# A deeper retention pipeline under the last projection pieces, and a last stage whose vector work runs by pairs of heads

## The chip, the cores and the metric

One core of a Trainium2 chip runs the whole program. The metric is the device time of one execution in microseconds (us); lower is better. The median of three executions of the kernel before is 3984.34 us (3983.41 to 3984.66). The engines are TensorE (PE, with its weight loads as PEld), VectorE (DVE), ScalarE (ACT), GpSimd (POOL) and SyncE (SP, which only issues loads here).

## What is computed

Two layers of a model with four parallel branches run over 18 tiles of 128 tokens (256 tokens of context, 2048 latent ones). Cut to what matters:

```python
h = rmsnorm(x) * (1 + scale) + shift
q, k, v, gate, ... = split(h @ w_in)          # 1024 -> 4096 columns
o_a, o_b = window attention, neighbourhood attention
o_c = retention(q, k, v)                      # linear attention with fixed decays, both ways
o_d = hgrn2(q, z_f, z_b, v)                   # the same with decays from the data, both ways
x = x + gate * rmsnorm(concat(o * silu(g)) @ w_out)
```

Each recurrence runs forwards and backwards and carries one 64x64 state per head. Within a 128-token tile, `o_c` is a product of queries and keys, masked by a fixed decay matrix, plus two products with the states. In `o_d` the decay differs in every channel, so the products of queries and keys inside a 64-token block are taken in seven levels (distances of 1, 2, 4, ... tokens), each with keys and queries scaled by its own decays. All data are fp32, and every matrix product is done in fp32.

## The kernel before

A layer has stages. A first stage projects 36 pieces (a piece is one tile by 512 columns, eight matmuls of 128x512). The window and neighbourhood attentions follow, with 72 further pieces laid between their matmuls and 4 projected ahead. The last two stages are the ones that the change touches.

**The retention stage** has `BACK_SLOTS` = 38 slots, numbered m. It projects the 32 pieces that are left, in alternation 6 (decays) and 7 (gates and values), in slots 0 to 33. `NO_PIECE = (6, 12)` leaves two slots without a piece, so `REST_END`, the last slot with one, is 33. TensorE works one piece ahead: the matmuls of the piece of slot m+1 fill the gaps of slot m (`fill`). Around them a slot holds

- in slots 0 to 17, one tile of the backward retention: `back_ret` on VectorE (rotate and decay the keys), the state product on TensorE, `back_state` on VectorE;
- in slots 2 to 37, half a tile of the backward hgrn2 (`back_hg_sums`, `decay_back`, `back_keys_hg`, `back_hg`). `BACK_AT` = 2 says where that begins;
- in slots 18 to 35 (`FORE` = 18), the forward retention tile j = m - 18: TensorE takes the state product (`keys_ret`) and the outputs of two pairs of heads (`outputs_ret`), VectorE subtracts the mean and adds up the state (`centred_ret`), and the tile after it is prepared: GpSimd rotates two tiles ahead (`rope_ret`), TensorE transposes (`turn_ret(j+1)`) and forms scores (`scores_ret(j+1)`) at the end of the slot, and VectorE masks the scores (`masked_ret(j)`) at the start of the next slot.

In slots 34 and 35 (`REST_END` + 1 and + 2) VectorE also makes the levels 0 to 1 and 2 to 6 of the first hgrn2 tile. In slot 36 TensorE forms its weights, and in slot 37 VectorE masks them.

**The last stage** runs over n = 1 to 19. In an iteration VectorE makes the seven levels of tile n (`level_hg`, four operations each, three in the last), and between them masks and adds up the level products of tile n-1 (`masked_hg`, once for each of four heads: one multiply of 448 columns out of PSUM, one reduction to 64), then finishes the residual of tile n-3 and the gating of tile n-1. ScalarE copies the weights of each head into one matrix (`weights_out`). GpSimd makes the decayed keys and the sum of both keys (`keys_hg`), clears the table of decays for tile n+1 (`clear_decays`), and stores results. TensorE forms the level products (`weights`), the outputs (`weigh`), transposes, and the output projection of tile n-2 (sixteen matmuls of 128x512, `fill` again).

Every engine runs its own queue in the order written, and waits on semaphores. `ps[:, 4:6]` holds the level products, one bank for each head of a pair, so a second pair waits until ScalarE has read the first.

Of the kernel before, what the change touches and what calls it, by code (L numbers as in the profile page):

```python
# [13 lines left out]
P = 128  # L14
# [162 lines left out]
NO_PIECE = (6, 12)  # L177
# [156 lines left out]
HG_CORE = 14 * GW + P + 2 * P + 4 * GW + 4 + 12 * P + 16 * P + 8 * LEVELS * P + 8 * P + 4 * P + 128 + (SLOTS + 1) * 64  # L334
# [20 lines left out]
def build(nc, ins, outs):  # L355
# [142 lines left out]
    with ExitStack() as s:  # L498
# [11 lines left out]
        hg.ks = sb(s, "hg_ks", [P, 2, 2, P])  # L510
# [4 lines left out]
        hg.w = sb(s, "hg_w", [P, SLOTS + 1, 64])  # L515
# [78 lines left out]
    for a, name in ((ret, "ret"), (hg, "hg")):  # L594
# [78 lines left out]
    def _(sp):  # L673
# [22 lines left out]
        for l in range(DEPTH):  # L696
# [217 lines left out]
            for m in range(BACK_SLOTS):  # L914
# [5 lines left out]
                if 0 <= m - FORE + 3 < NT:  # L920
                    load_ret(m - FORE + 3)
# [51 lines left out]
    def _(pool):  # L973
        for l in range(DEPTH):
# [156 lines left out]
            for n in range(NT + 3):  # L1131
# [13 lines left out]
    def _(pe):  # L1145
# [3 lines left out]
        for l in range(DEPTH):  # L1149
# [328 lines left out]
            def weights(t, g):  # L1478

                b, u = t % 2, l * NT + t  # L1480
                if g == 0:
                    pe.wait_ge(hg.qk_ready, u + 1)
                    pe.wait_ge(hg.ks_ready, u + 1)
# [15 lines left out]
                product(SLOTS, hg.ks[:, b, g], hg.xT[:, b, g])  # L1499
# [46 lines left out]
            for m in range(BACK_SLOTS):  # L1546
# [19 lines left out]
                if 0 <= j + 1 < NT:  # L1566
                    turn_ret(j + 1)
# [14 lines left out]
                if 0 <= j + 1 < NT:  # L1582
                    scores_ret(j + 1)
# [38 lines left out]
    def _(act):  # L1622
# [37 lines left out]
        for l in range(DEPTH):  # L1660
# [214 lines left out]
            def weights_out(t, h):  # L1875
                u = l * NT + t
                act.wait_ge(hg.tc_ready, HEADS * u + h + 1)
                need(act, hg.o_done, 2 * u + h // 2)
                for blk in range(2):
                    at, other = slice(blk * 64, (blk + 1) * 64), slice((1 - blk) * 64, (2 - blk) * 64)  # L1880
                    nc.scalar.activation(hg.p[at, h % 2, at], hg.tc[at, h % 2, :], ACT.Copy)
                    last = nc.scalar.activation(hg.p[at, h % 2, other], ps[at, 4 + h % 2, (SLOTS + 1) * 64:(SLOTS + 2) * 64],
                                                ACT.Copy)
                last.then_inc(hg.p_ready, 1)
# [13 lines left out]
            for m in range(BACK_SLOTS):  # L1898
# [8 lines left out]
                if 0 <= j + 1 < NT:  # L1907
                    take_ret(j + 1)
                if 0 <= j < NT:
                    square(j)  # L1910
                if REST_AT[m] and REST_AT[m][0] == 6:
                    bounds_ln(*REST_AT[m])
                if m in (REST_END + 1, REST_END + 2):
                    take_decays(m - REST_END - 1)
# [667 lines left out]
```

## Time and profile before

| what | value |
|---|---|
| time, median of three | 3984.34 us |
| the profiled execution: its time / its span | 3983.12 us / 3981.3 us |
| TensorE busy (share of the span) | 3793.2 us (95%) |
| VectorE busy | 2382.4 us (60%) |
| ScalarE busy | 1237.6 us (31%) |
| GpSimd busy | 572.8 us (14%) |
| first weights of the last stage masked, layer 2 | at 3542.62 us |
| one iteration of the last stage, VectorE | 3699.59 to 3722.70 us |

The profiled time lies 1.8 us above its span and 1.2 us below the median of the runs. Busy shares are means over stages with different limits, so the text reads the two changed stages in order of time. All starts are counted from the start of the span; the rows are of the second layer, whose code is that of the first.

### The profile page before, as it was taken

The numbers are of one execution on the slowest core, as the hardware profiler recorded it, in microseconds if no ns is written. First come the engines' busy times: TensorE is split into PE (matmuls) and PEld (weight loads), VectorE is DVE, ScalarE is ACT, GpSimd is POOL, SyncE is SP. The second block draws the span as 40 slices with busy tenths as digits, with TensorE's granted clock in tenths as the row PEclk, the third lists the DMA queues.
The fourth block names the chain that finished last, engine by engine and source line by source line (L and its number), as shares of the span: only waits on it lengthen the run. The fifth ranks groups of instructions, "written<-read, shape, count | busy, mean of one in ns | idle before, by whom it ended". The sixth has DMA issues, their size and how long they took to land. (4 is left out here: it accounts for less than half of the span.)

```text
span 3981.3 us, 63647 instructions
## 1 busy us (share of the span) xinstructions
PE 3793.2 (95%) x24449; PEld 2062.0 (52%) x24449; DVE 2382.4 (60%) x4811; ACT 1237.6 (31%) x3545; POOL 572.8 (14%) x870
## 2 busy tenths in 40 slices
PE   7999999999999998899999999999999989979998
PEld 4544555555554455555544455554555545555554
DVE  2334345224667887899932333551256688889996
ACT  3311232233331122445542023232333212224544
POOL 2000000100000354100100000001000005521100
PEclk9999999999999998999999999999999999979999
DMA  7432121222223334322332121213222233333322
GB/s 243 145 139 96 51 67 50 92 75 70 89 81 107 116 106 140 117 97 96 129 117 87 48 89 54 74 39 119 76 79 75 87 107 114 113 133 108 116 96 71
DMA packets 234365, 388.92 MB, mean 98 GB/s; under 512 B 30000, under 2 KB 150032, under 8 KB 233936
## 3 DMA queue, kind: packets, MB, share of 16 engines
q1 hardware_dynamic: 194096, 262.55, 20.8%
q0 software_dynamic: 39968, 122.30, 8.5%
q8 instruction: 195, 3.19, 0.3%
q14 instruction: 106, 0.87, 0.1%
HBM read 264.42 MB, written 122.25 MB: 97 GB/s over the span
## 5 line engine op out<-in xcount | busy, mean ns | idle before, releaser
L1184 PE MATMUL ps<-w_sb,hT 128*128 128x512 f32 x4608 | 2193.0, 609 | 3.7 <-ACT hT L1681 2.4
L1184 PEld LDWEIGHTS ps<-w_sb,hT 128*128 128x128 f32 x4608 | 812.5, 191 | 764.5 <-issue 725.7
L1539 PE MATMUL ps<-wo_sb,mT 128*128 128x512 f32 x1152 | 537.5, 606 | 3.4 <-ACT mT L1851 3.4
L980 POOL DMA_DIRECT2D projected<-row_t x252 | 138.6, 550 | 2461.4 <-DVE row_t L2087 1084.4
L2084 DVE RECIPROCAL e_t<-e_t 128x256 f32<-128x256 f32 (+1 forms) x180 | 430.7, 2393 | 6.2
L1539 PEld LDWEIGHTS ps<-wo_sb,mT 128*128 128x128 f32 x1152 | 207.1, 191 | 209.2 <-issue 198.1
L2082 DVE TENSOR_SCALAR e_t<-e_t 128x256 f32<-128x256 f32 (+1 forms) x180 | 71.3, 396 | 226.0 <-ACT row_t L1699 194.9
L1693 ACT ACTIVATE row_t<-ps 128x512 f32<-128x512 f32 x108 | 64.5, 597 | 393.5 <-PE ps L1184 387.8
L2191 DVE TENSOR_REDUCE nei_st<-ps 128x2 f32<-128x512 f32 x72 | 49.8, 691 | 209.7 <-PE ps L1294 209.7
L2224 DVE COPY win_pT<-ps 128x512 f32<-128x512 f32 x64 | 44.3, 692 | 213.2 <-PE ps L1303 213.2
L2224 DVE COPY nei_pT<-ps 128x512 f32<-128x512 f32 x64 | 44.3, 691 | 207.8 <-PE ps L1303 207.8
L2191 DVE TENSOR_REDUCE win_st<-ps 128x2 f32<-128x512 f32 x72 | 49.6, 689 | 189.9 <-PE ps L1294 189.9
L1754 ACT ACTIVATE win_pT<-ps 128x512 f32<-128x512 f32 (+1 forms) x128 | 64.5, 504 | 313.3 <-PE ps L1303 313.3
L2388 DVE TENSOR_TENSOR hg_q<-hg_d,hg_xT 128x256 f32<-128x256 f32 x252 | 152.1, 604 | 12.5 <-issue 6.1
L1754 ACT ACTIVATE nei_pT<-ps 128x512 f32<-128x512 f32 (+1 forms) x136 | 74.4, 547 | 243.7 <-PE ps L1303 243.7
L1303 PEld LDWEIGHTS ps<-ident,nei_e 128*128 128x128 f32 x736 | 92.9, 141 | 105.9 <-issue 103.3
L1698 ACT ACTIVATE e_t<-ps 128x256 f32<-128x256 f32 x108 | 41.3, 382 | 317.1 <-PE ps L1184 316.3
L1303 PEld LDWEIGHTS ps<-ident,win_e 128*128 128x128 f32 x656 | 83.6, 141 | 102.2 <-issue 100.2
L2423 DVE TENSOR_REDUCE hg_tc<-hg_w 128x64 f32<-128x448 f32 x144 | 133.3, 925 | 4.9
L2064 DVE TENSOR_SCALAR xt<-xt,stat 128x1024 f32<-128x1024 f32 x36 | 27.0, 752 | 178.6 <-ACT stat L1669 178.6
L1321 PEld LDWEIGHTS ps<-win_v,win_pT 128*64 128x64 f32 x2624 | 92.0, 137 | 73.8 <-issue 73.2
L1110 POOL DMA_DIRECT2D out_streams<-y_t x36 | 21.0, 584 | 691.4 <-DVE y_t L2451 691.4
(248 smaller groups left out, 5405.3 us busy)
## 6 DMA issues: line engine op xcount, KB each, us to landing
projected<-row_t POOLq DMA_DIRECT2D x288, 256.0 KB, 2.7
w_sb<-in_w_in SPq DMA_DIRECT2D x14, 2048.0 KB, 9.2
hg_raw<-projected SPq DMA_DIRECT2D x72, 256.0 KB, 4.9
out_streams<-y_t POOLq DMA_DIRECT2D x36, 512.0 KB, 4.0
wa<-in_w_ada SPq DMA_DIRECT2D x10, 1536.0 KB, 7.8
hg_braw<-projected SPq DMA_DIRECT2D x108, 128.0 KB, 2.4
hg_raw<-projected SPq DMA_DIRECT2D x36, 384.0 KB, 5.2
mx_t<-mixed SPq DMA_DIRECT2D x36, 384.0 KB, 4.5
```

Source lines behind the costliest of these rows:

```text
L980: pool.dma_start(rows[tok(t), g * GRP:(g + 1) * GRP], row_t[:, p.slot]).then_inc(row_stored[p.slot], 16)
L1184: mm = nc.tensor.matmul(ps[:, p.bank, :], hT[:, k, t * P:(t + 1) * P], w_sb[:, g % 2, k, :], start=(k == 0), stop=(k == KC - 1))
L1303: last = nc.tensor.transpose(ps[:, TURN_BANK, i * P:(i + 1) * P], a.e[:, u % 2, hp, c * P:(c + 1) * P], ident[:, :])
L1321: last = nc.tensor.matmul(ps[half * HD:(half + 1) * HD, OUT_BANK, h * HD:(h + 1) * HD], a.pT[:, f, at:at + HD], values_of(tau, h)[c], star ...
L1539: mm = nc.tensor.matmul(ps[:, 6 + g, :], mT[:, t % 2, k, :], wo_sb[:, k, g * GRP:(g + 1) * GRP], start=(k == 0), stop=(k == KC - 1))
L1754: nc.scalar.activation(a.pT[:, f, 0:n], ps[:, TURN_BANK, 0:n], ACT.Copy).then_inc(taken_act, 1)
L2082: own.mark(nc.vector.tensor_scalar(e, e, 1.0, None, ALU.add))
L2084: own.mark(nc.vector.reciprocal(e, e))
L2191: own.mark(nc.vector.reduce_max(st[:, MX, pair_at], both[:, :, n:n + CTX], AX_X))
L2224: nc.vector.tensor_copy(a.pT[:, 1, 0:n], ps[:, TURN_BANK, 0:n]).then_inc(taken_dve, 1)
L2388: own.mark(nc.vector.tensor_tensor(halves(q), halves(d, size + s, TO_END * size), halves(x), ALU.mult))
L2423: nc.vector.tensor_reduce(hg.tc[:, h % 2, :], hg.w[:, :, :].rearrange("p s n -> p n s"), AX_X, ALU.add).then_inc(hg.tc_ready, 1)
```

## The change

- `NO_PIECE` becomes empty: the 32 pieces stand in slots 0 to 31, `REST_END` is 31 and `BACK_AT` 0, so the backward hgrn2 runs in slots 0 to 35.
- The forward retention is prepared one step further ahead. GpSimd rotates tile j+3 in a slot; TensorE transposes tile j+2 behind the outputs and forms the scores of tile j+1 at the start of the slot, not at its end; VectorE masks the scores of tile j+1 straight behind `centred_ret(j)`.
- The levels of the first hgrn2 tile are split 0 to 3 and 4 to 6, in slots 32 and 33; ScalarE puts `square` behind the copies there, and GpSimd clears the decays before `rope_ret`.
- In the last stage `masked_hg` and `weights_out` take a pair of heads at a time. The decayed keys and the sum of both keys are made by VectorE, at the end of the levels; `keys_hg` is gone from GpSimd. ScalarE takes the transposed decays and x before `take_y`.

The core of the diff:

```diff
-NO_PIECE = (6, 12)
+NO_PIECE = ()
...
-                if 0 <= m - FORE + 3 < NT:
-                    load_ret(m - FORE + 3)
+                if 0 <= m - FORE + 4 < NT:
+                    load_ret(m - FORE + 4)
...
+                if 1 <= j + 1 < NT:
+                    scores_ret(j + 1)
                 if 0 <= j < NT:
                     keys_ret(j)
                     outputs_ret(j, 0)
...
-                if 0 <= j + 1 < NT:
-                    turn_ret(j + 1)
+                if j + 1 == 0:
+                    turn_ret(0)
+                elif 2 <= j + 2 < NT:
+                    turn_ret(j + 2)
...
+                    own.mark(last)
+                    own.wait()
+                    nc.vector.tensor_tensor(hg.xT[:, b, 4:6], hg.xT[:, b, 4:6], hg.xT[:, b, 2:4], ALU.add).then_inc(hg.qk_ready, 1)
...
+            def keys_hg(t):
+
+                b, u = t % 2, l * NT + t
+                need(dve, hg.kv_done, u - 1)
+                nc.vector.tensor_tensor(hg.kd[:, b], hg.ed[:, b], hg.raw[:, b, 5 * GW:6 * GW], ALU.mult).then_inc(hg.kf_ready, 1)
+
+            def masked_hg(t, g):
+
+                u, n = l * NT + t, (SLOTS + 1) * 64
+                dve.wait_ge(hg.p_done, HEADS * u + 2 * g + 2)
+                need(dve, hg.tc_ready, 2 * u + g)
+                own.mark(nc.vector.tensor_tensor(hg.w[:, :, :, :].rearrange("p h s n -> p h (s n)"), ps[:, 4:6, 0:n],
...
             for m in range(BACK_SLOTS):
                 j = m - FORE
                 piece = REST_AT[m]
-                if 0 <= j < NT:
-                    masked_ret(j)
                 if piece:
                     gates(*piece)
...
                 if 0 <= j < NT:
                     centred_ret(j)
+                if 0 <= j + 1 < NT:
+                    masked_ret(j + 1)
...
-                    for lv in range(0, 2):
+                    for lv in range(0, 4):
                         level_hg(0, lv)
                 if m == REST_END + 2:
-                    for lv in range(2, LEVELS):
+                    for lv in range(4, LEVELS):
                         level_hg(0, lv)
                     edges_hg(0)
+                    keys_hg(0)
...
                 if 2 <= n <= NT:
                     masked_hg(n - 1, 0)
-                    masked_hg(n - 1, 1)
```

How instructions stand on the engines, at three places. On TensorE, a forward slot of the retention stage before: `ret_kd` is the state product of tile j, `ret_p`, `ret_sf` and `ret_sb_all` are its outputs, `ret_x` the transposes and `ret_xT` the scores of tile j+1, `w_sb` the piece.

```order
L1363 MATMUL ps<-ret_raw,ret_kd 64x64 x4
L1432 MATMUL ps<-ret_raw,ret_p 128x64 x2
L1436 MATMUL ps<-ret_sf,ret_qd 128x64 x2
L1439 MATMUL ps<-ret_sb_all,ret_qd 128x64 x2
L1184 MATMUL ps<-w_sb,hT 128x512 x2
L1432 MATMUL ps<-ret_raw,ret_p 128x64 x2
L1436 MATMUL ps<-ret_sf,ret_qd 128x64 x2
L1439 MATMUL ps<-ret_sb_all,ret_qd 128x64 x2
L1363 MATMUL ps<-hg_braw,hg_bkd 64x64 x4
L1399 MATMUL ps<-ident,ret_x 128x128 x4
L1184 MATMUL ps<-w_sb,hT 128x512 x2
L1411 MATMUL ps<-ret_xT 128x128 x4
```

The same queue and place with the change, where the scores are of tile j+1 and the transposes at the end of tile j+2:

```order
L1397 MATMUL ps<-ret_xT 128x128 x4
L1349 MATMUL ps<-ret_raw,ret_kd 64x64 x4
L1418 MATMUL ps<-ret_raw,ret_p 128x64 x2
L1422 MATMUL ps<-ret_sf,ret_qd 128x64 x2
L1425 MATMUL ps<-ret_sb_all,ret_qd 128x64 x2
L1170 MATMUL ps<-w_sb,hT 128x512 x2
L1418 MATMUL ps<-ret_raw,ret_p 128x64 x2
L1422 MATMUL ps<-ret_sf,ret_qd 128x64 x2
L1425 MATMUL ps<-ret_sb_all,ret_qd 128x64 x2
L1354 MATMUL ps<-hg_braw,after 128x256
L1356 MATMUL ps<-ones,hg_braw 128x1 x2
L1385 MATMUL ps<-ident,ret_x 128x128 x4
```

The scores moved from behind the outputs of their predecessor to ahead of its state product, and between the transposes and the scores of one tile there is now most of a slot. On VectorE, the weighing of the first pair of heads in an iteration of the last stage, before (`hg_w` is the masked product, `hg_tc` its sum):

```order
L2397 TENSOR_TENSOR hg_d<-hg_d 128x2x128
L2402 TENSOR_TENSOR hg_d<-hg_d 128x2x128
L2419 TENSOR_TENSOR hg_w<-ps,keep 128x448
L2423 TENSOR_REDUCE hg_tc<-hg_w 128x64
L2419 TENSOR_TENSOR hg_w<-ps,keep 128x448
L2423 TENSOR_REDUCE hg_tc<-hg_w 128x64
L2388 TENSOR_TENSOR hg_q<-hg_d,hg_xT 128x256
```

And with the change:

```order
L2390 TENSOR_TENSOR hg_d<-hg_d 128x2x128
L2397 TENSOR_TENSOR hg_d<-hg_d 128x2x128
L2420 TENSOR_TENSOR hg_w<-ps,keep 128x896
L2424 TENSOR_REDUCE hg_tc<-hg_w 128x128
L2381 TENSOR_TENSOR hg_q<-hg_d,hg_xT 128x256
```

Two operations stand where four stood, over the same elements, twice in an iteration. The end of the levels on VectorE before (`hg_total` and `hg_qx` are made by `edges_hg`, `y_t` by the residual):

```order
L2402 TENSOR_TENSOR hg_d<-hg_d 128x2x4x32
L2388 TENSOR_TENSOR hg_q<-hg_d,hg_xT 128x256
L2389 TENSOR_TENSOR hg_k<-hg_d,hg_xT 128x256
L2402 TENSOR_TENSOR hg_d<-hg_d 128x2x2x64
L2409 COPY hg_total<-hg_d 128x2
L2410 TENSOR_TENSOR hg_qx<-hg_d,hg_xT 128x512
L2448 SCALAR_TENSOR_TENSOR y_t<-y_t,y_stat,gp_sb 128x1024
```

And with the change:

```order
L2397 TENSOR_TENSOR hg_d<-hg_d 128x2x4x32
L2381 TENSOR_TENSOR hg_q<-hg_d,hg_xT 128x256
L2382 TENSOR_TENSOR hg_k<-hg_d,hg_xT 128x256
L2394 TENSOR_TENSOR hg_xT<-hg_xT 128x256
L2397 TENSOR_TENSOR hg_d<-hg_d 128x2x2x64
L2404 COPY hg_total<-hg_d 128x2
L2405 TENSOR_TENSOR hg_qx<-hg_d,hg_xT 128x512
L2413 TENSOR_TENSOR hg_kd<-hg_ed,hg_raw 128x256
L2449 SCALAR_TENSOR_TENSOR y_t<-y_t,y_stat,gp_sb 128x1024
```

Two operations of 256 columns came to VectorE, the sum of the keys (L2394) and the decayed keys (L2413).

## Rows read from the trace of the kernel before

**Rows 1.** Timeline of TensorE, slots 2, 4, 12 and 17 (start us, us, engine, line)
```profile
3183.97 0.45 PE L1363 MATMUL ps<-ret_braw,ret_bkd 128*64 128x64 f32 x8
...
3200.32 0.45 PE L1363 MATMUL ps<-ret_braw,ret_bkd 128*64 128x64 f32 x8
...
3262.56 0.69 PE L1363 MATMUL ps<-ret_braw,ret_bkd 128*64 128x64 f32 x8 [6.89 <-DVE ret_bkd L2294]
...
3306.51 0.45 PE L1363 MATMUL ps<-ret_braw,ret_bkd 128*64 128x64 f32 x8 [0.65 <-DVE ret_bkd L2294]
```

**Rows 2.** Timeline of TensorE, forward slots 18, 20, 28, 31 and 33
```profile
3315.77 0.45 PE L1363 MATMUL ps<-ret_raw,ret_kd 128*64 128x64 f32 x8
...
3339.11 0.45 PE L1363 MATMUL ps<-ret_raw,ret_kd 128*64 128x64 f32 x8
...
3438.28 0.66 PE L1432 MATMUL ps<-ret_raw,ret_p 128*128 128x64 f32 x4 [1.16 <-DVE ret_p L2335]
...
3474.38 0.45 PE L1363 MATMUL ps<-ret_raw,ret_kd 128*64 128x64 f32 x8
...
3498.92 0.45 PE L1363 MATMUL ps<-ret_raw,ret_kd 128*64 128x64 f32 x8
```

**Rows 3.** Timeline of TensorE, slots 35 and 36, behind the last piece
```profile
3524.10 1.12 PE L1432 MATMUL ps<-ret_raw,ret_p 128*128 128x64 f32 x4 [5.12 <-DVE ret_p L2335]
...
3539.50 1.56 PE L1492 MATMUL ps<-hg_q,hg_k 64*64 64x64 f32 x48 [5.75 <-DVE hg_k L2389]
```

**Rows 4.** Timeline of VectorE, slots 35 and 37
```profile
3528.41 0.42 DVE L2346 TENSOR_REDUCE ret_st<-ps 128x4 f32<-128x256 f32 x1 [4.36 <-PE ps L1439]
...
3530.97 0.42 DVE L2388 TENSOR_TENSOR hg_q<-hg_d,hg_xT 128x256 f32<-128x256 f32 x1
...
3542.62 0.62 DVE L2419 TENSOR_TENSOR hg_w<-ps,keep 128x448 f32<-128x448 f32 x1
```

**Rows 5.** Windows: busy us of each engine (instructions), PEclk, DMA share, GB/s
```profile
3520.00:3540.00 20.00, 10.14 (x69) 8.74 (x73) 14.99 (x38) 2.97 (x8) 2.40 (x4) 0.66 0.32 124
```

**Rows 6.** Timeline of VectorE, one iteration of the last stage
```profile
3699.59 1.28 DVE L2448 SCALAR_TENSOR_TENSOR y_t<-y_t,y_stat,gp_sb 128x1024 f32<-128x1024 f32 x1
...
3702.84 2.02 DVE L2388 TENSOR_TENSOR hg_q<-hg_d,hg_xT 128x256 f32<-128x256 f32 x1
...
3706.09 0.62 DVE L2419 TENSOR_TENSOR hg_w<-ps,keep 128x448 f32<-128x448 f32 x1
3706.74 0.93 DVE L2423 TENSOR_REDUCE hg_tc<-hg_w 128x64 f32<-128x448 f32 x1
...
3709.28 0.41 DVE L2388 TENSOR_TENSOR hg_q<-hg_d,hg_xT 128x256 f32<-128x256 f32 x1
3709.61 0.42 DVE L2389 TENSOR_TENSOR hg_k<-hg_d,hg_xT 128x256 f32<-128x256 f32 x1
3710.06 0.43 DVE L2397 TENSOR_TENSOR hg_d<-hg_d 128x256 f32<-128x256 f32 x1
...
3722.70 1.28 DVE L2448 SCALAR_TENSOR_TENSOR y_t<-y_t,y_stat,gp_sb 128x1024 f32<-128x1024 f32 x1
```

**Rows 7.** Timeline of GpSimd, the same iteration
```profile
3703.12 0.74 POOL L1103 TENSOR_TENSOR hg_kd<-hg_ed,hg_raw 128x256 f32<-128x256 f32 x1
3703.81 0.73 POOL L1105 TENSOR_TENSOR hg_ks<-hg_xT 128x256 f32<-128x256 f32 x1
```

**Rows 8.** Timeline of TensorE, the same iteration
```profile
3700.28 2.84 PE L1539 MATMUL ps<-wo_sb,mT 128*128 128x512 f32 x6
...
3710.52 0.63 PE L1517 MATMUL ps<-hg_raw,hg_p 128*128 128x64 f32 x4 [0.99 <-ACT hg_p L1882]
...
3718.51 0.70 PE L1451 MATMUL ps<-hg_raw,past 128*128 128x256 f32 x2 [0.32 <-ACT hg_d L1839]
...
3723.36 1.99 PE L1539 MATMUL ps<-wo_sb,mT 128*128 128x512 f32 x4
```

**Rows 9.** The page, DMA issues: KB each, median us to landing
```profile
hg_raw<-projected SPq DMA_DIRECT2D x72, 256.0 KB, 4.9
```

More of the change, by code:

```diff
@@ L514, in build @@
         wo_sb = sb(s, "wo_sb", [P, KC, D_MODEL])
-        hg.w = sb(s, "hg_w", [P, SLOTS + 1, 64])
+        hg.w = sb(s, "hg_w", [P, 2, SLOTS + 1, 64])
         hg.p = sb(s, "hg_p", [P, 2, P])
@@ L1124, in _ @@
                     clear_decays(1)
+                if 0 <= m - FORE + 3 < NT:
+                    rope_ret(m - FORE + 3)
+                if 0 <= m - FORE - 2 < NT:
+                    gate_ret(m - FORE - 2)
             pool.wait_ge(ret.sf_ready, (l + 1) * NT)
@@ L1498, in weights @@
                     product(lv, hg.k[:, b, lv, g], hg.q[:, b, lv, g])
-                product(SLOTS, hg.ks[:, b, g], hg.xT[:, b, g])
+                product(SLOTS, hg.xT[:, b, 4 + g], hg.xT[:, b, g])
                 product(SLOTS + 1, hg.k[:, b, LEVELS - 1, g], hg.q[:, b, LEVELS - 1, g])
@@ L1873, in scaled, with weights_out @@
                 last.then_inc(hg.out_ready, 1)
-            def weights_out(t, h):
+            def weights_out(t, g):
                 u = l * NT + t
-                act.wait_ge(hg.tc_ready, HEADS * u + h + 1)
-                need(act, hg.o_done, 2 * u + h // 2)
+                act.wait_ge(hg.tc_ready, 2 * u + g + 1)
+                need(act, hg.o_done, 2 * u + g)
                 for blk in range(2):
                     at, other = slice(blk * 64, (blk + 1) * 64), slice((1 - blk) * 64, (2 - blk) * 64)
[L1881 to L1884, printed above, removed]
+                    nc.scalar.activation(hg.p[at, :, at], hg.tc[at, :, :], ACT.Copy)
+                    last = nc.scalar.activation(hg.p[at, :, other], ps[at, 4:6, (SLOTS + 1) * 64:(SLOTS + 2) * 64], ACT.Copy)
+                last.then_inc(hg.p_ready, 2)
             def take_y(t, g):
@@ L1906, in _ @@
                     decay_back(i)
-                if 0 <= j + 1 < NT:
-                    take_ret(j + 1)
-                if 0 <= j < NT:
+                if j + 1 == 0:
+                    take_ret(0)
+                    take_ret(1)
+                if 0 <= j < NT and m <= REST_END:
                     square(j)
+                if 2 <= j + 2 < NT:
+                    take_ret(j + 2)
                 if REST_AT[m] and REST_AT[m][0] == 6:
@@ L1916, in _ @@
                     take_keys(m - REST_END - 1)
+                if 0 <= j < NT and m > REST_END:
+                    square(j)
                 if m == BACK_SLOTS - 1:
@@ L1937, in _ @@
                     scale_y(n - 3)
+                if n + 1 < NT:
+                    take_decays(n + 1)
+                    take_x(n + 1)
                 if n >= 2:
@@ L1950, in _ @@
                 if l + 1 < DEPTH and n == NT + 1:
-                    for used, count in ((hg.o_done, 2 * NT), (hg.ks_ready, NT), (hg.kf_ready, NT), (hg.out_ready, NT), (hg.s_saved, 64)):
+                    for used, count in ((hg.o_done, 2 * NT), (hg.kf_ready, NT), (hg.out_ready, NT), (hg.s_saved, 64)):
                         act.wait_ge(used, count * (l + 1))
@@ L2532, in _ @@
             if l + 1 < DEPTH:
-                for used, count in ((hg.o_done, 2 * NT), (hg.ks_ready, NT), (hg.kf_ready, NT), (hg.p_ready, HEADS * NT), (hg.s_saved, 64)):
+                for used, count in ((hg.o_done, 2 * NT), (hg.p_ready, HEADS * NT), (hg.s_saved, 64)):
                     dve.wait_ge(used, count * (l + 1))
```

55 lines of the change are left out of this document (13 added, 42 removed).

## The prediction, made before the changed kernel ran

> **What bounds the kernel now.** The busy shares of the page say TensorE (95%), but the changed code lies in the last two stages of each layer, and these have limits of their own. So I read the timeline of TensorE through the retention stage first, then what ended its waits, then one iteration of the last stage on every engine.
>
> The retention stage is bound by TensorE while it has pieces to project. Two backward slots take 3200.32 - 3183.97 = 16.35 us with no idle time worth naming [rows 1]. From slot 2 to slot 17 it is 3306.51 - 3183.97 = 122.5 us, 15 slots of 8.17 us. Two of these slots have no piece, and still the mean is that of a full slot (16.35 / 2 = 8.18): in slot 12 TensorE waits 6.89 us for VectorE's decayed keys [rows 1], because the backward recurrence, not the piece, then sets the time. **An empty slot costs as much as a full one.** In the forward half two slots take 3339.11 - 3315.77 = 23.34 us where TensorE never waits, 11.67 a slot [rows 2]. The 13 slots from 18 to 31 take 3474.38 - 3315.77 = 158.6 us against 13 x 11.67 = 151.7: some 7 us go to waits of 1.16 us for the masked scores, one in nearly every second slot, and to what they bring with them.
>
> Behind the last piece (slot 33 on) nothing fills the gaps. From 3498.92 [rows 2] to the first masked weights at 3542.62 [rows 4] it is 43.7 us for three forward tiles and the levels of the first hgrn2 tile. TensorE waits 5.12 us for masked scores that stand behind two levels on VectorE, and 5.75 us for the last level [rows 3]; VectorE waits 4.36 us for the outputs [rows 4]. The work goes from one to the other and back.
>
> The last stage is bound by VectorE: between the two residuals there is no gap, 3722.70 - 3699.59 = 23.11 us [rows 6]. TensorE needs 3723.36 - 3700.28 = 23.08 us for the same iteration, with waits of 0.99 and 0.32 us in it [rows 8]. Without them it needs 21.77 us. So this is how far an iteration can fall, whatever VectorE saves.
>
> **Retention stage, slots without a hole.** The backward slots keep their 8.17 us: VectorE does the same work for each, and the pieces now sit where TensorE only waited. Two more pieces are done by slot 17, so the last is done by slot 31, and two forward slots of 11.67 us lose their cover. The backward hgrn2 starts two slots earlier. Its operations are the same and its loads keep their distance of two slots behind the pieces that they read, so I cost it at nothing; the pieces on TensorE hide it, and without them it is some 0.8 us once (two operations of 256 columns at 0.41 [rows 6]).
>
> **Deeper pipeline.** Scores of tile j+1 are masked right behind `centred_ret(j)`, so the products need nothing that VectorE has still to do in their slot: the waits of 1.16 us go, and slots 18 to 30 take 152 us. What is late next could be GpSimd: it now waits for the state product of the next slot before it can decay the keys three tiles ahead, and the store of a piece stands behind that. The store has three row buffers, so I take nothing.
>
> **The uncovered part** is the largest unknown. It now holds five forward tiles (slots 31 to 35), the levels, and the first weights. VectorE's work for a tile: the mean, the state, the sums and the scaling take 3530.97 - 3528.41 = 2.6 us [rows 4], the mask and the two products for the decayed queries some 1.3 (three operations of between 0.33 and 0.65 from start to start [rows 6]): 3.9 us. Levels: five took 3539.50 - 3530.97 = 8.5 us [rows 3, 4], so seven take 12, with edges and keys 13.5. Together 5 x 3.9 + 13.5 = 33 us. To this come waits. The outputs of a tile take 3528.41 - 3524.10 = 4.3 us there [rows 3, 4], and in slots 34 and 35, where no level covers them, VectorE waits for them; before the first level some 4 us for transposes and copies; at the end 1.6 us for the first weights. 33 + 2 x 4.3 + 4 + 1.6 = 47 us. Why the levels in halves matter: the masked scores no longer stand behind them, so TensorE's outputs run under the levels.
>
> TensorE runs this part with a granted clock of 0.66 in the mean, between its two levels of 1.2 and 2.4 GHz; ahead of it are waits of some us in which it is hardly used [rows 5]. I leave that clock in the sum. The Trainium skill ("TensorE: Matmul & The Clock Gate", Part 1, on the oscillation) says that an array that waits falls back to half rate and starts each burst cold. This speaks against moving two more tiles out from under the pieces, and the trace agrees: 0.66 where the pieces are gone. With a full clock the five tiles would take about 42 us in place of 47; by the rule it stays 47.
>
> From slot 18 to the first masked weights: now 3542.62 - 3315.77 = 226.9 us; then 152 + 47 = 199. **28 us a layer.** Bounds: 40 us for the uncovered part gives 35; the price of today's uncovered tiles, (43.7 - 13.5) / 3 = 10.1 us each, gives 5 x 10.1 + 13.5 = 64 and leaves 11.
>
> **Last stage, VectorE.** Three terms for an iteration.
>
> - GpSimd's two operations go. They run from 3703.12 to 3704.54 [rows 7], and `hg_q`, started at 3702.84, takes 2.02 us where the same operation takes 0.41 a little later [rows 6]: -1.6 us. If clearing the decays, which stays on GpSimd, holds it for as long as one of the two (0.7), it is -0.9.
> - Weighing by pairs. Today a pair of heads takes 3709.28 - 3706.09 = 3.19 us. From 256 columns (0.41) to 448 (0.62) an operation grows by 1.1 ns a column with 0.13 us fixed. Twice the columns: the multiply 1.1 us, and the reduction, if only its fixed part is saved, 0.93 + 0.80 = 1.73. The pair then takes 2.8: -0.4, twice: -0.8. Bounds: nothing, or -1.4 if the reduction grows only by the 1.1 ns a column.
> - Two operations come: one behind a wait (0.45 from start to start, as 3709.61 to 3710.06) and one without (0.33, as 3709.28 to 3709.61) [rows 6]: +0.8.
>
> 23.1 - 1.6 - 0.8 + 0.8 = 21.5 us, bounds 20.9 and 23.0 (23.1 - 0.9 + 0.8). TensorE's 21.77 is above 21.5, so TensorE becomes the bound, and its wait of 0.32 us goes by ScalarE's new order. I take 21.9 for the handover between two engines that are so close. That is 1.2 us less in each of the 15 iterations n = 3 to 17; n = 1 gains the same, n = 2 is TensorE's already, and n = 18 and 19 have no levels: 19.2 us a layer. TensorE could use the first pair's weights from 3710.52 - 0.99 = 3709.5 [rows 8]; today VectorE begins their mask at 3706.09 [rows 6], late by its own queue, and once it runs ahead it begins as soon as the products are there, so I take no wait. What waits longer is the load of the keys two tiles ahead, now released by `hg_kd` at the end of VectorE's iteration (about 3721) and not by GpSimd at 3703.86. It lands in 4.9 us [rows 9] and is needed about 15 us into the next iteration of TensorE, near 3738: 12 us of slack.
>
> On contention the Trainium skill ("GPSIMD Engine Reference", section 1) says that GpSimd shares its SBUF interfaces with VectorE, and names instructions with two SBUF inputs or in a 2-port mode. The trace agrees: `hg_q` has two SBUF inputs. Were the long `hg_q` due to something else and stayed, the iteration would be 23.1 us and only the retention stage would gain, 56 us in all.
>
> **Sum.** 2 layers x (28 + 19.2) = 94.4 us. From the profiled execution's own 3983.1 (its span plus 1.8) this is 3888.7; the median lies 1.2 higher: 3889.9. The fixed stall of n = 3, where VectorE waits for decays that GpSimd clears behind the two operations that go, gives about 1.4 (two operations of 0.7 [rows 7]) a layer more: **3887 us**.
>
> **Rivals.**
>
> - *Uncovered tiles stay dear* (0.14). The outputs need the state that VectorE adds up after the last outputs, so a chain across two engines stays, and the half clock makes it longer. For it: 10.1 us a tile today. Against: part of that was scores behind levels (5.12 us [rows 3]), which goes. 64 in place of 47 us: 34 us later, 3921.
> - *VectorE stays the bound of the last stage* (0.13): reduction in proportion, or the clearing of the decays in the way, 22.3 to 23.0 us an iteration. 12 to 33 us later, 3899 to 3920.
> - *More than forecast* (0.09): the uncovered part at 40 us and TensorE at its 21.77 everywhere: 3864 to 3869.
> - *No change to speak of* (0.01): VectorE falls behind in the back slots without the holes, and both stages keep their time.
> - *Slower* (0.03). The load of the keys has moved from the start of an iteration to its end. Should it take over 17 us to land, TensorE's transposes wait, and with them VectorE's next levels. Each us beyond costs 1 us in each of 16 iterations and both layers; from 3 us on (20 us to land) the gain of 97 us is gone, and at 23 us the time is about 4080. Against it: 4.9 us to land in a stage that moves little [rows 9].
> - The forecast itself: 0.60, with a range of its own of 3869 to 3904.
>
> The 8 in 10 range takes in the forecast, most of both milder rivals and of the faster one: 3864 to 3920. A change of 0.2%, 8 us, is about what a measurement of this kernel can tell from none. Faster by more than that 0.96, within it 0.01, slower 0.03.
>
> **What would show it.** Slots 2 to 17 still 122 us, now with no wait of several us for `ret_bkd`; no wait for `ret_p` in slots 18 to 30, two slots 23.3 us; 45 to 50 us from the state product of slot 31 to the first `hg_w`; `hg_q` at 0.41 us and `hg_w` at 1.1, `hg_tc` at 1.7; an iteration of 21.8 to 22.0 us, with VectorE waiting a few tenths for the level products. Wrong would be: a `hg_q` that stays long, an `hg_tc` over 1.8, a wait of TensorE for `hg_raw` from a DMA, over 8 us from tile to tile in slots 33 to 35 beyond the levels, or waits for `ret_kd`.

## The result, and the profile after

The changed kernel takes 3874.39 us in the median of three (3872.44 to 3875.03), against 3984.34 us before: 0.9723 of the time, 95% interval 0.9701 to 0.9746, 110 us less. The profiled execution has a span of 3870.5 us against 3981.3, 110.8 less. The forecast was 3887 us, with a range of 3864 to 3920. Of all executions told below one was out of line, the second of keys_pool with 8744 us beside 3903 to 3905, and its ratio leaves that one out.

The retention stage first, as in [rows 1, 2]: TensorE's timeline of the second layer, slots 2, 17, 18, 19, 20, 30 and 31.

```profile
3127.11 0.45 PE L1349 MATMUL ps<-ret_braw,ret_bkd 128*64 128x64 f32 x8
...
3251.45 0.45 PE L1349 MATMUL ps<-ret_braw,ret_bkd 128*64 128x64 f32 x8 [1.50 <-DVE ret_bkd L2287]
...
3261.74 0.45 PE L1349 MATMUL ps<-ret_raw,ret_kd 128*64 128x64 f32 x8
...
3273.46 0.45 PE L1349 MATMUL ps<-ret_raw,ret_kd 128*64 128x64 f32 x8
...
3284.69 0.45 PE L1349 MATMUL ps<-ret_raw,ret_kd 128*64 128x64 f32 x8
...
3399.41 0.45 PE L1349 MATMUL ps<-ret_raw,ret_kd 128*64 128x64 f32 x8
...
3409.41 0.45 PE L1349 MATMUL ps<-ret_raw,ret_kd 128*64 128x64 f32 x8
```

Slots 2 to 17 take 124.3 us, with no wait of several us. Two forward slots take 22.95 us and hold no wait for `ret_p`. The 13 slots from 18 to 31 take 147.7 us, where before they took 158.6 [rows 2].

Then the uncovered part, as in [rows 3, 4]. TensorE waits for a copy of ScalarE in slot 32, for VectorE to mask the scores before (`ret_p`) in slot 34, for its centred outputs (`att_out`) in slot 35, and at the end for the state:

```profile
3417.86 1.22 PE L1397 MATMUL ps<-ret_xT 64*128 64x128 f32 x8 [4.48 <-ACT ret_xT L1806]
...
3441.36 1.22 PE L1397 MATMUL ps<-ret_xT 64*128 64x128 f32 x8 [5.74 <-DVE ret_p L2328]
...
3451.14 0.69 PE L1349 MATMUL ps<-ret_raw,ret_kd 128*64 128x64 f32 x8 [1.95 <-DVE att_out L2352]
...
3458.24 1.56 PE L1477 MATMUL ps<-hg_q,hg_k 64*64 64x64 f32 x48 [0.98 <-DVE ret_sf L2346]
```

VectorE's timeline of the same stretch has two waits of some us, in slots 32 and 35, and ends with the first masked weights:

```profile
3423.94 0.42 DVE L2339 TENSOR_REDUCE ret_st<-ps 128x4 f32<-128x256 f32 x1 [4.50 <-PE ps L1425]
...
3456.68 0.42 DVE L2339 TENSOR_REDUCE ret_st<-ps 128x4 f32<-128x256 f32 x1 [3.42 <-PE ps L1425]
...
3460.51 1.09 DVE L2420 TENSOR_TENSOR hg_w<-ps,keep 128x896 f32<-128x896 f32 x1
```

From slot 31 to `hg_w` it is 3460.51 - 3409.41 = 51.1 us, and from slot 18 198.8 us, against 226.9 before. The windows of the covered slots, the uncovered part and the last stage (columns as in [rows 5], PEclk third from the end):

```profile
3261.74:3409.41 147.67, 147.67 (x869) 88.52 (x867) 118.42 (x222) 34.36 (x89) 82.22 (x104) 1.00 0.35 113
3409.41:3460.51 51.10, 36.90 (x328) 31.65 (x328) 40.10 (x100) 11.78 (x33) 21.24 (x30) 0.65 0.57 192
3480.00:3850.00 370.00, 369.31 (x3598) 215.58 (x3588) 338.17 (x648) 173.60 (x584) 17.51 (x33) 1.00 0.30 106
```

The clock is full where pieces cover the waits, and 0.65 in the mean where nothing does, as before [rows 5]. In the last stage TensorE is busy for 369.3 of 370 us. One iteration there, first on VectorE, as in [rows 6]:

```profile
3605.06 1.28 DVE L2449 SCALAR_TENSOR_TENSOR y_t<-y_t,y_stat,gp_sb 128x1024 f32<-128x1024 f32 x1
...
3608.30 0.47 DVE L2381 TENSOR_TENSOR hg_q<-hg_d,hg_xT 128x256 f32<-128x256 f32 x1
...
3610.02 1.08 DVE L2420 TENSOR_TENSOR hg_w<-ps,keep 128x896 f32<-128x896 f32 x1
3611.14 1.69 DVE L2424 TENSOR_REDUCE hg_tc<-hg_w 128x128 f32<-128x896 f32 x1
...
3624.71 0.42 DVE L2394 TENSOR_TENSOR hg_xT<-hg_xT 128x256 f32<-128x256 f32 x1
...
3626.18 0.42 DVE L2413 TENSOR_TENSOR hg_kd<-hg_ed,hg_raw 128x256 f32<-128x256 f32 x1
3626.52 1.27 DVE L2449 SCALAR_TENSOR_TENSOR y_t<-y_t,y_stat,gp_sb 128x1024 f32<-128x1024 f32 x1
```

and on TensorE, as in [rows 8]:

```profile
3605.65 2.84 PE L1524 MATMUL ps<-wo_sb,mT 128*128 128x512 f32 x6
...
3614.44 0.45 PE L1349 MATMUL ps<-hg_raw,hg_kd 128*64 128x64 f32 x8
3614.82 0.66 PE L1502 MATMUL ps<-hg_raw,hg_p 128*128 128x64 f32 x4
...
3620.65 1.88 PE L1524 MATMUL ps<-wo_sb,mT 128*128 128x512 f32 x4
3622.37 0.59 PE L1437 MATMUL ps<-hg_raw,past 128*128 128x256 f32 x2
...
3627.11 2.84 PE L1524 MATMUL ps<-wo_sb,mT 128*128 128x512 f32 x6
```

Both give 21.46 us, and neither engine shows a wait. `hg_q` takes 0.47 us where it took 2.02 [rows 6].

**Where the 110.8 us came from.** Up to the first weights of layer 1 the spans differ by 1592.79 - 1565.66 = 27.1 us. From there to slot 2 of layer 2 it is 1591.2 us before and 1561.5 after, 29.7 less. In the retention stage of layer 2 (slot 2 to `hg_w`) it is 358.65 - 333.40 = 25.3 us, and behind it 438.7 - 410.0 = 28.7. So the retention stages gave 52 us (56 forecast), and the last stages 58 (41 forecast). The 29.7 also hold the stages of layer 2 that the change doesn't touch.

### The profile page after: what moved, and what is told of

Same layout as the page of the kernel before. It is cut to its first block, busy times and chain, and to the rows that moved or that the text cites. A ratio compares the mean times of both kernels' runs of the same rounds, so it can differ in the third digit from the quotient of the medians.

```text
span 3870.5 us, 62967 instructions
## 1 busy us (share of the span) xinstructions
PE 3759.0 (97%) x24449; PEld 2057.6 (53%) x24449; DVE 2311.2 (60%) x4739; ACT 1186.4 (31%) x3257; POOL 515.0 (13%) x798
## 3 DMA queue, kind: packets, MB, share of 16 engines
q1 hardware_dynamic: 194096, 262.55, 21.9%
## 4 chain that ended last, share of the span: by engine, by line
PE 91%; DVE 5%; SPq 1%; DMA 1%; issue 1%; ACT 1%; POOL 0%; DVEq 0%; ACTq 0%; POOLq 0%
PE ps L1170 51%; PE ps L1524 13%; PE ps L1307 6%; PE ps L1289 4%; PE ps L1276 3%; PE ps L1280 2%; PE ps L1477 2%; PE ps L1439 2%; PE ps L1349 1%; PE ps L1236 1%; PE ps L1418 1%; PE ps L1502 1%; DVE e_t L2077 1%; PE ps L1182 1%; PE ps L1506 1%
## 5 line engine op out<-in xcount | busy, mean ns | idle before, releaser
L2075 DVE TENSOR_SCALAR e_t<-e_t 128x256 f32<-128x256 f32 (+1 forms) x180 | 62.2, 346 | 207.9 <-ACT row_t L1689 186.3
L2424 DVE TENSOR_REDUCE hg_tc<-hg_w 128x128 f32<-128x896 f32 x72 | 122.3, 1698 | 2.5
L1307 PE MATMUL ps<-win_v,win_pT 128*64 128x64 f32 x2624 | 118.5, 229 | 0.3 <-DVE win_pT L2217 0.3
L1289 PE MATMUL ps<-ident,nei_e 128*128 128x128 f32 x736 | 113.4, 273 | 1.7 <-ACT nei_pT L1744 1.4
```

Of the source, the lines that this page charges most:

```text
L1289: last = nc.tensor.transpose(ps[:, TURN_BANK, i * P:(i + 1) * P], a.e[:, u % 2, hp, c * P:(c + 1) * P], ident[:, :])
L1307: last = nc.tensor.matmul(ps[half * HD:(half + 1) * HD, OUT_BANK, h * HD:(h + 1) * HD], a.pT[:, f, at:at + HD], values_of(tau, h)[c], star ...
L2424: nc.vector.tensor_reduce(hg.tc[:, :, :], hg.w[:, :, :, :].rearrange("p h s n -> p h n s"), AX_X, ALU.add).then_inc(hg.tc_ready, 1)
```

## The experiments

The experiments come in three groups, and in each the kernel before ran beside the others (medians 3982.9, 3987.9 and 3984.3 us), so times are told as ratios to it, each with a 95% interval that reaches 0.0010 to 0.0017 to either side, up to 7 us; a difference between two ratios is uncertain by more. The changed kernel was measured apart from them, at 0.9723, and its own interval reaches 0.0023 (9 us). Where a few us matter, the traces decide: in each kernel with the deep pipeline, slot 18 to `hg_w` of layer 1 and of layer 2 agree within 0.6 us.

### Which part gives what

**ret_only** is the kernel before with the parts of the diff for the retention stage: `NO_PIECE`, the pipeline one step deeper, the order of `clear_decays` and `square`, and the new split of the levels. Like fill_only and single_heads below it keeps the larger buffer of `hg_w` and the wait for `ret.scaled` of the changed kernel. Of its diff:

```diff
-                    for lv in range(0, 2):
+                    for lv in range(0, 4):
```

> The kernel before with the retention-stage part alone (32 pieces in slots 0 to 31, the deeper pipeline, levels 0 to 3 and 4 to 6); the last stage weighs single heads and GpSimd makes the keys, as before. Theory from the two traces: of the 110.8 us between the spans the retention stages hold 51.7 us, so 3932 us (3928 to 3936). Rival, the terms of the forecast (28 us a layer): 3928. Rival, the parts need each other (the levels of the first tile or the released queues gain only together): above 3940.

Measured: 0.9875 (0.986 to 0.989), which on 3984.3 us is 50 us less, 3934.5. That fits the theory's 3932 and speaks against the rival above 3940, which the interval just touches; it doesn't separate 3932 from 3928.

**last_only** is the kernel before with the other parts, among them

```diff
-                    masked_hg(n - 1, 0)
-                    masked_hg(n - 1, 1)
+                    masked_hg(n - 1, 0)
```

> The kernel before with the last-stage part alone (pairs of heads, keys on VectorE, ScalarE's order); the retention stage keeps its two empty slots and the shallow pipeline. Theory from the two traces: the last stages hold 59.1 us of the difference, so 3925 us (3921 to 3929), with 21.46 us an iteration. Rival, the terms of the forecast (21.9 us an iteration, 20.6 us a layer): 3943.

Measured: 0.9846 (0.9831 to 0.986), 61 us less, 21.48 us an iteration in the mean. The rival with 21.9 us, 3943, is ruled out. The two parts add up: 50 + 61 = 111 us, against 110 for both. They don't need each other, and the last stage gives the larger part: the two ratios alone hardly separate 61 from 50, but the spans of the changed kernel say the same, 58 and 52.

### Filled slots and depth

**fill_only** is the kernel before with one line changed:

```diff
-NO_PIECE = (6, 12)
+NO_PIECE = ()
```

> The kernel before with NO_PIECE empty and nothing else: five forward tiles lie behind the last piece, in the shallow pipeline, and levels 0 to 1 and 2 to 6. Theory: the depth of the pipeline, not the filled slots, makes the uncovered tiles cheap; at 10.1 us a tile as before, slot 18 to the first masked weights is 158.6 + 64 = 222.6 us against 226.9: 4.3 us a layer, 3975 us (3968 to 3984). Rival, filling the slots is what gains: as in the changed kernel (51 us uncovered), 3940 to 3950.

Measured: 0.9983 (0.9973 to 0.9993), 7 us less.

**holes** is the changed kernel with the line put back:

```diff
-NO_PIECE = ()
+NO_PIECE = (6, 12)
```

> The changed kernel with NO_PIECE = (6, 12) back: 32 pieces in slots 0 to 33, three forward tiles uncovered, all else as changed. Theory: a covered slot costs 11.35 us and an uncovered tile some 8 (3.9 of VectorE and a wait), so two tiles more under the pieces cost 2 x 3.4 = 7 us a layer: 3888 us (3880 to 3896). Rival, uncovered tiles cost the 10.1 us of the kernel before: 2.5 us a layer, 3879. Rival, filling brings nothing once the pipeline is deep: 3874.

Measured: 0.9771 (0.9757 to 0.9786), 19 us more than the changed kernel's ratio gives. The slots of layer 2, from the starts of their state products (`ret_kd`), in us:

| kernel | 18 to 31 | 31 | 32 | 33 | 34 | 35 to `hg_w` | all |
|---|---|---|---|---|---|---|---|
| before | 158.6 | 11.4 | 13.1 | 6.9 | 12.7 | 24.1 | 226.9 |
| fill_only | 157.3 | 6.8 | 12.8 | 17.1 | 18.3 | 9.4 | 221.7 |
| holes | 149.4 | 11.2 | 10.0 | 8.5 | 10.0 | 20.3 | 209.4 |
| changed | 147.7 | 9.6 | 10.7 | 12.8 | 8.6 | 9.4 | 198.8 |

Filling alone takes 5.2 us off (5.7 in layer 1), depth alone 17.5, both 28.1. "Depth" here is all of the change but the filling. The last stage's part acts in this stretch too, by some 1 us: ret_only, which lacks it, takes 200.2 in place of 198.8 (200.0 and 199.1 in layer 1). In the old pipeline the stretch is less steady than in the deep one: 224.1 us in layer 2 of last_only, and 226.7 in layer 1. In the shallow pipeline five uncovered tiles cost 64.4 us, just the 64 that today's 10.1 us a tile gave. TensorE's timeline of fill_only, slots 33 and 34, shows why:

```profile
3497.60 1.11 PE L1432 MATMUL ps<-ret_raw,ret_p 128*128 128x64 f32 x4 [7.62 <-DVE ret_p L2335]
...
3516.10 1.12 PE L1432 MATMUL ps<-ret_raw,ret_p 128*128 128x64 f32 x4 [9.03 <-DVE ret_p L2335]
```

The masked scores stand behind the levels, and TensorE can do nothing until they come. In the deep pipeline the scores of the next tile are masked ahead of them. That this order, and not the earlier rotation and transposes, makes the difference is read from the waits; no run took it alone. In the deep pipeline the two filled slots save 60.0 - 51.1 = 8.9 us behind slot 31 and 1.7 before it: two tiles under pieces cost 149.4 + 11.2 + 10.0 - 147.7 = 22.9 us, and uncovered 51.1 - 38.8 = 12.3 (38.8 is slot 33 to `hg_w` of holes), some 6.2 a tile. I had expected 8. A tile behind the pieces is cheap only if its chain is short.

### The levels in halves

**levels_2_5** puts the old split back into the changed kernel:

```diff
-                    for lv in range(0, 4):
+                    for lv in range(0, 2):
...
-                    for lv in range(4, LEVELS):
+                    for lv in range(2, LEVELS):
```

> The changed kernel with the levels of the first hgrn2 tile split as before, 0 to 1 in slot 32 and 2 to 6 in slot 33. Theory: the 5.74 us wait for masked scores behind four levels goes, one behind five levels comes a slot later, and the wait of 3.42 us in slot 35 stays: the same or up to 2 us a layer longer, 3874 to 3878. Rival, the halves are what made the uncovered tiles cheap: 4 us a layer or more, above 3882.

Measured: 0.9718 (0.9701 to 0.9734), no difference. The long wait of TensorE moved by a slot, as its timeline of this kernel shows:

```profile
3443.48 0.71 PE L1397 MATMUL ps<-ret_xT 64*128 64x128 f32 x8 [2.32 <-DVE ret_p L2328]
...
3456.69 0.69 PE L1349 MATMUL ps<-ret_raw,ret_kd 128*64 128x64 f32 x8 [6.27 <-DVE att_out L2352]
```

and VectorE's:

```profile
3462.24 0.42 DVE L2339 TENSOR_REDUCE ret_st<-ps 128x4 f32<-128x256 f32 x1 [3.43 <-PE ps L1425]
```

5.74 us behind four levels and 1.95 behind three are now 2.32 behind two and 6.27 behind five; VectorE still waits 3.43 us in slot 35, where no level covers the outputs. The sum of TensorE's two waits grew from 7.7 to 8.6 us, and slot 18 to `hg_w` from 198.8 to 199.4. The halves bring next to nothing.

**spread** has a third stretch of levels:

```diff
-                    for lv in range(0, 4):
+                    for lv in range(0, 2):
...
                 if m == REST_END + 2:
+                    for lv in range(2, 4):
+                        level_hg(0, lv)
+                if m == REST_END + 3:
                     for lv in range(4, LEVELS):
```

> The changed kernel with the levels of the first hgrn2 tile in three slots: 0 to 1, 2 to 3, 4 to 6 in slots 32, 33 and 34. Theory: VectorE waits 3.42 us in slot 35 since no level covers TensorE's outputs there; with levels in slot 34 the wait goes: 3 us a layer, 3867 to 3870. Rival, the last level then holds up the first weights: 3874 or more.

Measured: 0.9703 (0.9688 to 0.9717), a span of 3865.9 us. Slot 18 to `hg_w` takes 196.2 us in place of 198.8, and 196.0 in place of 199.1 in layer 1. VectorE's wait of 3.42 us is gone; its two long ones left are both in slot 32, ahead of the first level:

```profile
3422.82 0.42 DVE L2339 TENSOR_REDUCE ret_st<-ps 128x4 f32<-128x256 f32 x1 [4.50 <-PE ps L1425]
...
3429.67 0.42 DVE L2357 TENSOR_REDUCE ret_st<-ret_o_sq 128x4 f32<-128x256 f32 x1 [2.31 <-ACT ret_o_sq L1812]
```

**copy_first** moves one operation of ScalarE in slot 31:

```diff
-                if 0 <= j < NT and m <= REST_END:
+                if 0 <= j < NT and m < REST_END:
                     square(j)
...
-                if 0 <= j < NT and m > REST_END:
+                if 0 <= j < NT and m >= REST_END:
                     square(j)
```

> The changed kernel with ScalarE's square behind the copy of the transposes in slot 31 too. Theory: the wait of 4.48 us of TensorE in slot 32 is that copy behind the square, which waits for the mean behind the last gates; without it 1 to 4 us a layer, 3866 to 3872. Rival, VectorE's gates of the last piece bound this slot: 3874.

Measured: 0.9718 (0.9703 to 0.9732), and 199.3 us from slot 18 to `hg_w` (198.8 in layer 1): nothing. The copy comes early now, and TensorE waits just as long at the same place, for VectorE:

```profile
3416.01 1.23 PE L1397 MATMUL ps<-ret_xT 64*128 64x128 f32 x8 [4.25 <-DVE ret_p L2328]
```

The rival held: `ret_p` stands behind the gates of the last piece, and ScalarE's copy was only the last of two late releasers.

**copy_spread** has both edits. 

> Both edits, the copy ahead of the square and the levels in three slots. If the two waits are independent: the sum of both, 4 to 7 us a layer, 3860 to 3866.

Measured: 0.9698 (0.9683 to 0.9712), a span of 3864.7 us, 196.0 us from slot 18. That is spread's time: my expected sum was too high by the part of copy_first. It is the fastest version by its ratio, but its interval overlaps the changed kernel's. What the traces show is 3 us a layer, from spread.

### What bounds the last stage

**dve_less** takes 1.1 us from VectorE in an iteration:

```diff
-                nc.vector.tensor_tensor(y_t[:, b], y_t[:, b], xo_t[:, b], ALU.add).then_inc(y_ready, 1)
+                nc.vector.tensor_tensor(y_t[:, b, 0:64], y_t[:, b, 0:64], xo_t[:, b, 0:64], ALU.add).then_inc(y_ready, 1)
```

> The changed kernel with the last addition of the residual over 64 of 1024 columns, which leaves out x in the other 960; VectorE saves 1.1 us in each iteration of the last stage. Theory A, TensorE bounds the last stage at 21.46 us (busy 369.3 of 370 us): no change, 3873 to 3875. Theory B, VectorE bounds it: down to TensorE's floor, by up to 1.1 us an iteration, 3840 to 3865.

Measured: 0.9711 (0.9696 to 0.9725), a span of 3871.7 us. VectorE's timeline of this kernel, from residual to residual:

```profile
3606.94 1.28 DVE L2449 SCALAR_TENSOR_TENSOR y_t<-y_t,y_stat,gp_sb 128x1024 f32<-128x1024 f32 x1
...
3611.89 1.09 DVE L2420 TENSOR_TENSOR hg_w<-ps,keep 128x896 f32<-128x896 f32 x1 [0.84 <-PE ps L1477]
...
3628.39 1.28 DVE L2449 SCALAR_TENSOR_TENSOR y_t<-y_t,y_stat,gp_sb 128x1024 f32<-128x1024 f32 x1
```

The iteration stays (21.45 here, 193.16 / 9 = 21.46 in the mean of nine), and VectorE now waits for the level products. Nine iterations as a window, TensorE busy in all of it:

```profile
3606.94:3800.10 193.16, 193.16 (x1912) 113.77 (x1910) 178.47 (x362) 92.45 (x307) 9.61 (x18) 1.00 0.33 114
```

**dve_more** adds 0.45 us to VectorE:

```diff
+                own.mark(nc.vector.tensor_tensor(hg.kd[:, b], hg.ed[:, b], hg.raw[:, b, 5 * GW:6 * GW], ALU.mult))
+                own.wait()
                 nc.vector.tensor_tensor(hg.kd[:, b], hg.ed[:, b], hg.raw[:, b, 5 * GW:6 * GW], ALU.mult).then_inc(hg.kf_ready, 1)
```

> The changed kernel with the product for hg_kd made twice, so VectorE has one more operation with a wait (0.45 us) in each iteration. Theory A, TensorE bounds and VectorE has slack s below 0.45: less than 14 us longer. Theory B, VectorE bounds: 0.45 x 16 x 2 = 14 us, 3889, with an iteration of 21.91 us.

Measured: 0.9746 (0.973 to 0.9762), a span of 3882.2 us, 11.7 more than the changed kernel's. The residuals on VectorE's timeline:

```profile
3613.03 1.28 DVE L2451 SCALAR_TENSOR_TENSOR y_t<-y_t,y_stat,gp_sb 128x1024 f32<-128x1024 f32 x1
...
3634.97 1.28 DVE L2451 SCALAR_TENSOR_TENSOR y_t<-y_t,y_stat,gp_sb 128x1024 f32<-128x1024 f32 x1
```

21.94 us, all of the 0.45 and a little more. Each theory holds for one side: 21.46 us is TensorE's floor, and VectorE has no slack beneath it. Less work on VectorE gains nothing, more costs at once. The total grew by less than 14 x 0.48 x 2 = 13.4 us: in either layer the step behind the residual of n = 17 got 0.9 us shorter (13.4 to 12.4).

**keys_pool** has GpSimd's two operations back:

```diff
+                nc.gpsimd.tensor_tensor(hg.kd[:, b], hg.ed[:, b], hg.raw[:, b, 5 * GW:6 * GW], ALU.mult).then_inc(hg.kf_ready, 1)
...
+                nc.gpsimd.tensor_tensor(hg.ks[:, b], hg.xT[:, b, 2:4], hg.xT[:, b, 4:6], ALU.add).then_inc(hg.ks_ready, 1)
```

> The changed kernel with hg_kd and hg_ks made by GpSimd again at the start of an iteration, and not by VectorE. Theory (GpSimd's two operations stretch hg_q from 0.41 to 2.02 us): VectorE loses 1.6 us and saves 0.8 in an iteration, 22.3 in place of 21.46 us, and the stall of n = 3 returns: 13 to 15 us a layer, 3902 us (3896 to 3906), with hg_q at 2.0 us. Rival, the stretch has another cause: hg_q stays at 0.47 and TensorE stays the bound, 3874.

Measured: 0.9793 (0.9777 to 0.9809), 28 us more, 22.24 us in most iterations. VectorE and GpSimd, start of an iteration:

```profile
3631.38 2.01 DVE L2396 TENSOR_TENSOR hg_q<-hg_d,hg_xT 128x256 f32<-128x256 f32 x1
...
3631.66 0.74 POOL L1103 TENSOR_TENSOR hg_kd<-hg_ed,hg_raw 128x256 f32<-128x256 f32 x1
3632.36 0.72 POOL L1105 TENSOR_TENSOR hg_ks<-hg_xT 128x256 f32<-128x256 f32 x1
```

`hg_q` ends at 3633.39, 0.3 us behind GpSimd's second operation. The contention was the right cause, and the price is the 1.6 us forecast, less the 0.8 of the two operations. The stall of n = 3 is back as well: VectorE stands idle for 3.06 us ahead of its first `hg_q` there, as in the kernel before, and for 1.65 in the changed one.

**single_heads** weighs one head at a time on both engines:

```diff
-                    masked_hg(n - 1, 0)
+                    masked_hg(n - 1, 0)
+                    masked_hg(n - 1, 1)
```

> The changed kernel with masked_hg and weights_out for one head at a time. From rows: a pair 1.09 + 1.70 us, two heads 3.19, so 0.4 us twice an iteration. If VectorE bounds the iteration it is 22.3 us: 3900 us (3895 to 3904). If TensorE does and VectorE has slack: less, down to 3876.

Measured: 0.9794 (0.9779 to 0.9808), 28 us more, 22.37 us in most iterations, 0.91 more where 0.8 was expected.

ScalarE's new order, which the forecast credited with TensorE's wait of 0.32 us, is in every run that has the last stage's part, and no run took it away alone. What speaks for it: such a wait stood 31 times in the kernel before, 9.7 us in all, and keys_pool and single_heads, where VectorE is the slower engine again, have 3 and 4 of them left, 0.9 and 1.2 us in all.

## Why the prediction was right, and where its terms were off

**Right.** The gain, its size within 13 us of 110, both stages that give it, and for the last stage what causes it. The backward slots kept their time within 2 us (124.3 against 122.5 forecast as unchanged; 123.9 against 125.4 before in layer 1). Filled slots cost what empty ones did. Slots 18 to 30 lost their waits for `ret_p`. `hg_q`, `hg_w` and `hg_tc` came out at 0.47, 1.08 and 1.70 us, where 0.41, 1.1 and 1.73 were forecast. The load of the keys held up nobody: TensorE shows no wait for it. So the slower rival had nothing to stand on.

**The step that failed: TensorE's floor.** "Without them it needs 21.77 us" took the two waits of [rows 8], 0.99 and 0.32, off 23.08. The floor is 21.46. Two more rows of TensorE in the kernel before say where the difference is:

```profile
3709.07 0.45 PE L1363 MATMUL ps<-hg_raw,hg_kd 128*64 128x64 f32 x8
...
3716.31 1.88 PE L1539 MATMUL ps<-wo_sb,mT 128*128 128x512 f32 x4
```

From the product with `hg_kd` to the first weighing [rows 8] it is 3710.52 - 3709.07 = 1.45 us, and after the change 3614.82 - 3614.44 = 0.38: the wait shown as 0.99 cost 1.07. From the four matmuls to the transposes it is 3718.51 - 3716.31 = 2.20, and after 3622.37 - 3620.65 = 1.72: the wait shown as 0.32 cost 0.48. The rest, some 0.1, is in what follows the transposes. In these rows an idle time is counted from a modelled end, and matmuls that follow one another without a wait overlap (starts 0.38 apart, each "0.45" long); a wait costs that overlap too. This fits the Trainium skill ("Perfetto Trace Analysis", per-instruction lifecycle), by which TensorE's end times are an estimate and not observed.

The next sentence, "TensorE becomes the bound", came true at a lower level, and so did VectorE's 21.5: the two meet within 0.05 us (dve_more's 21.94 less the 0.45 added is 21.49). The 21.9 "for the handover between two engines that are so close" was a surcharge without a row, and none is paid. Between the residuals of n = 3 and n = 17 that is 14 x 0.44 x 2 = 12 us. The head of the stage, from the first `hg_w` to the first residual, took 64.9 us before and takes 58.7: 6.2 less, where n = 1 and n = 3 with its stall were put at 3.8 and n = 2 at nothing. In layer 1 it fell from 65.4 to 57.9, by 7.5. That is 6 us more in two layers. The stall of n = 3 gave its 1.4 (3.06 to 1.65); what had been left out are VectorE's waits for TensorE ahead of it, 1.48 and 1.55 us before in layer 2, of which 0.73 is left. 12 and 6 make the last stages' gain 60 us out of 41; 1.3 us of it is lost between the last residual of layer 1 and slot 2 of layer 2, which leaves the 58. Less the 4 us that the retention stages fell short, these are the 13 us of the miss.

**The retention stage: a right sum of two wrong terms.** 28 us from slot 18 to the first weights were forecast, and 28.1 (27.9 in layer 1) measured. That it fits so well is luck: one term was 4 us too high and the other 4 too low. The covered slots took 147.7 and not 152: two slots take 22.95 us in the new order and not 23.34, and the last of the 13 takes 10.0, since no matmuls of a piece stand at the head of slot 31. The uncovered part took 51.1 and not 47. Its waits on VectorE are 9.9 us (4.5, 3.4, and 2.0 for ScalarE), where 8.6 and 4 were put in; its work is 41.2 us, where 3.9 a tile, 13.5 for the levels and 1.6 make 34.6. Two things were left out. The gates of the last piece lie in it, from 3410.87 to 3414.45, 3.6 us. And GpSimd rotates two tiles and gates outputs there, and stretches part of what it meets, which I put at the other 3 us without a run that tests it; this row of VectorE shows one case, a product of four columns that takes 0.17 us elsewhere in the same stretch (3450.11):

```profile
3414.90 1.27 DVE L2341 TENSOR_SCALAR ret_st<-ret_st 128x4 f32<-128x4 f32 x1
```

The 4 us by which the stages missed 56 lie ahead of slot 18: the step from 17 to 18 takes 10.3 us and not 9.3, in both layers, and slots 2 to 17 take 1.5 us less in layer 1 and 1.8 more in layer 2. Why is open.

**Why the levels in halves matter** was wrong as a reason. By the order of the code the scores come out from behind the levels because `masked_ret(j+1)` stands behind `centred_ret(j)`; the split moved the wait by one slot (levels_2_5), and a third stretch would have gained (spread).

**The clock** in the uncovered part was 0.65, as left in the sum. Both levels show in the rows: eight matmuls for the scores take 1.22 us at 3441.36 of the changed kernel and 0.71 at 3443.48 of levels_2_5. No run warmed the whole part, so what the clock costs there stays an estimate.

**Rivals.** *Uncovered tiles stay dear* was decided by depth: with the old pipeline it would have come true to 0.4 us (fill_only). *VectorE stays the bound* is half true, since it is level with TensorE. *More than forecast* came true by half: TensorE is at its own floor, and that is 0.3 us lower than it was thought to be, but the uncovered part took 51.1 us and not the 40 of this rival.

## What to carry to other kernels

Before taking work out from under a long filler, shorten the chain that will then stand bare: filling two slots was worth 5 us a layer in the shallow pipeline and some 10 in the deep one. A small vector operation on the busy engine can be cheaper than the same on GpSimd, if the trace shows a neighbour stretched beside it: 0.8 us paid, 1.6 saved. To find an engine's floor, don't subtract the waits that the profile shows, but count start to start over a stretch without any; and when two engines come out level, test both sides, a little less and a little more, before working on either.

## What the runs showed of the hardware

- Some VectorE operations that meet a two-input GpSimd operation end only about when that has ended: `hg_q` at 3633.39 beside two that end at 3633.08, and `ret_st` at 3416.17 beside one that ends at 3416.13. It isn't the size that counts: four columns took 1.27 us. But not all are held. GpSimd's clearing of 512 columns (0.54 us) stretched `hg_q` and the `hg_k` behind it by 0.06 to 0.07 only. Beside a GpSimd product (`ret_kd`, 3410.02 to 3410.68) a reduction of VectorE with its one input in SBUF, at 3410.12, took its usual 0.41 us, and so did a product of two inputs that had started ahead of GpSimd's (`hg_bkd`, at 3409.78). And VectorE operations that read PSUM ran beside a rotation without loss (`att_out` 0.41 and `ret_p` 0.67 us at 3416.46 and 3416.80, where GpSimd's `ret_x` ran from 3416.22 to 3417.49). The Trainium skill ("GPSIMD Engine Reference", section 1) names two SBUF inputs or a 2-port mode. The rows agree for `hg_q`, the reduction and the operations that read PSUM; `ret_st` has one input, and no trace here shows whether it runs in a 2-port mode.
- A reduction over an inner axis with a stride of 64 grew from 0.93 us for 448 columns to 1.70 for 896, 1.7 ns a column, where the multiply in front of it grew from 0.62 to 1.08, 1.0 ns a column. In the durations, joining two heads saves only fixed parts, 0.16 us in either.
